# Levels 2 to 4 of a triangular inverse as one finite series, in a two-layer hybrid decoder on one Trainium2 core

## What is computed

```python
def step(state, inp):
    rt, wt, kt, vt, kkt, at = inp
    sa = jnp.einsum('bhvk,bhk->bhv', state, -kkt)
    state = state * wt[:, :, None, :] + sa[..., None] * (kkt * at)[:, :, None, :] + vt[..., None] * kt[:, :, None, :]
    return state, jnp.einsum('bhvk,bhk->bhv', state, rt)
```

```python
s = jnp.einsum('bhcqd,bhckd->bhcqk', q[:, :, :, q0:kend], k[:, :, :, :kend]).astype(jnp.float32) * scale
p = jax.nn.softmax(jnp.where(mask, s, -jnp.inf), axis=-1)
w = p[:, :, 0] - lam * p[:, :, 1]
```

## Time and profile before

| what | value |
|---|---|
| three runs | 2528.36, 2528.58, 2529.15 us |
| profiled execution | 2529.05 us, its span 2527.2 us |
| PE busy | 99% of the span |
| DVE, ACT, POOL busy | 75%, 48%, 19% |
| mean granted TensorE clock | 0.997 |
| chain that ended last | PE 94%, DVE 3%, issue 1%, ACT 1% |
| idle of PE before transposes (L1438) that wait for DVE L1149 | 2.3 us in 8 times |
| one even step (L1475 at 112.42 us to L1475 at 165.24 us) | 52.82 us |

### The profile page before, as it was taken

One profiled execution on the slowest core, in us unless ns is written; L12 is line 12 of the kernel. 1 busy time (PEld: TensorE's weight loads), 2 busy tenths in 40 slices (PEclk: granted clock), 3 DMA queues, 4 the chain that ended last, 5 costly groups with the idle time before them and its releaser, 6 DMA issues.

```text
span 2527.2 us, 49529 instructions
## 1 busy us (share of the span) xinstructions
PE 2495.7 (99%) x18082; PEld 2223.5 (88%) x18082; DVE 1883.5 (75%) x3163; ACT 1202.7 (48%) x1717; POOL 468.8 (19%) x360
## 2 busy tenths in 40 slices
PE   8999999999999999999999999999999999999998
PEld 8999998788888888888888888888888888888887
DVE  7888888776665666566889999997666566755776
ACT  6555455454333343343556565655434334333345
POOL 0011000132210221022221212223222012200223
PEclk9999999999999999999999999999999999999999
DMA  7333332355555555555554444445555555555543
GB/s 269 111 128 121 136 115 99 143 185 189 191 189 194 183 188 194 184 190 183 175 200 155 177 151 177 153 155 205 186 186 190 192 183 193 188 186 193 188 166 133
DMA packets 66006, 437.36 MB, mean 173 GB/s; under 512 B 9456, under 2 KB 10864, under 8 KB 17904
## 3 DMA queue, kind: packets, MB, share of 16 engines
q1 hardware_dynamic: 62064, 435.25, 48.8%
q10 hardware_dynamic: 3840, 0.70, 0.1%
HBM read 433.82 MB, written 2.10 MB: 172 GB/s over the span
## 4 chain that ended last, share of the span: by engine, by line
PE 94%; DVE 3%; issue 1%; ACT 1%; POOL 0%; DMA 0%; DVEq 0%; SPq 0%; POOLq 0%; ACTq 0%
PE acc L324 51%; PE acc L376 21%; PE acc L359 9%; PE acc L321 7%; DVE w_low L314 1%; PE mixer_banks L1438 1%; PE mixer_banks L1726 0%; PE mixer_banks L1548 0%; PE mixer_banks L1730 0%; PE acc L336 0%; PE mixer_banks L1525 0%; PE mixer_banks L1496 0%; PE mixer_banks L1489 0%; POOL arena L528 0%; DMA w_raw<-w_even 0%
## 5 line engine op out<-in xcount | busy, mean ns | idle before, releaser
L309 ACT ACTIVATE w_high<-w_raw 128x1024 fp32r<-128x1024 f32 x839 | 855.0, 1056 | 887.2 <-PE acc L376 746.2
L314 DVE TENSOR_TENSOR w_low<-w_raw,w_high 128x1024 fp32r<-128x1024 f32 x840 | 1058.9, 1291 | 19.4 <-ACT w_high L309 17.9
L324 PE MATMUL acc<-h_split,w_high 128*128 128x512 f32 x3840 | 944.7, 393 | 0.0
L324 PEld LDWEIGHTS acc<-h_split,w_high 128*128 128x128 f32 x3840 | 700.2, 189 | 131.2
L504 POOL TENSOR_TENSOR arena<-arena,norm_scale 128x256 f32<-128x256 f32 x152 | 232.3, 1528 | 1354.3 <-DVE arena L398 1335.6
L324 PE MATMUL acc<-mix_split,w_high 128*128 128x512 f32 x1904 | 463.0, 393 | 0.8 <-DVE x_residual L966 0.7
L324 PEld LDWEIGHTS acc<-mix_split,w_high 128*128 128x128 f32 x1904 | 348.0, 189 | 67.0 <-issue 1.7
L398 DVE TENSOR_REDUCE arena<-acc 128x256 f32<-128x512 f32 x240 | 165.5, 690 | 286.3 <-PE acc L376 270.0
L376 PEld LDWEIGHTS acc<-h_split,w_low 128*128 128x128 f32 x2752 | 352.8, 192 | 13.4
L376 PE MATMUL acc<-h_split,w_low 128*128 128x256 f32 x2752 | 357.1, 283 | 0.0
L359 PE MATMUL acc<-h_split,w_low 128*128 128x256 f32 x1824 | 276.4, 283 | 0.0
(11 more groups left out here) (289 smaller groups left out, 1600.6 us busy)
## 6 DMA issues: line engine op xcount, KB each, us to landing
w_raw<-w_gu SPq DMA_DIRECT2D x176, 1024.0 KB, 4.8
w_raw<-w_down SPq DMA_DIRECT2D x64, 1024.0 KB, 4.9
w_raw<-w_odd SPq DMA_DIRECT2D x64, 1024.0 KB, 4.8
w_raw<-w_even SPq DMA_DIRECT2D x49, 1024.0 KB, 4.8
w_raw<-w_down SPq DMA_DIRECT2D x32, 768.0 KB, 4.2
w_raw<-w_odd_out SPq DMA_DIRECT2D x12, 1024.0 KB, 4.8
w_raw<-w_even_out SPq DMA_DIRECT2D x10, 1024.0 KB, 4.7
w_raw<-w_even_out SPq DMA_DIRECT2D x6, 896.0 KB, 4.4
```

The source lines that it names most:

```text
L309: act.activation(wh[:, self.res, ks], raw[:, self.raw, ks], ACT.Copy).then_inc(high_done, 1)
L314: dve.tensor_tensor(wl[:, self.res, ks], raw[:, self.raw, ks], wh[:, self.res, ks].bitcast(F32), ALU.subtract).then_inc(low_done, 1)
L324: pe.matmul(acc[self.acc][:, 0:2 * T], wh[:, self.res, k], flat(both), start=k == 0, stop=stop)
```

## The change

In even steps levels 2 to 4 become one finite series. Let X be minus the inverse of the 4x4-block part times the rest of L within the 32x32 blocks. X is nilpotent, its eighth power is zero, and so the inverse is (I + X)(I + X²)(I + X⁴) times the start. `z(2)` makes X from one mask (`C_OVER`, the sum of the three masks of levels 2 to 4). `txt(2)` and `txt(3)` each hold two groups of 16 products: one squares the power (`pe.matmul(bank(1)...Xb...Zs)`), one multiplies T. `txt(4)` is one group. `z(3)` and `z(4)` are gone. DVE transposes each power before its square (`power_turned`), and T is only transposed back after level 4. POOL lays on two masks instead of four. The dense pieces are 5, 6, 6, 6, 6, 4, 3, 3, 3 tiles instead of 5, seven times 4, 3, 3, 3: 42 in both. `kbT` moves from ahead of a dense piece to between `z(6)` and R0, `at_oT` from behind `txt(5)` to behind `txt(6)`, and the banks of `kbn`, R0, U0 and `at_oT` change.

```diff
@@ POOL
                 pool.wait_ge(S["rw_L"], 4 * j + 4)
-                for l in range(1, LEVELS - 2):
...
-                    pool.tensor_tensor(Xb[:, l % 2], Ld, bc(half_mask(l), 4), ALU.mult).then_inc(S["rw_X"], 1)
+                pool.wait_ge(S["rw_TXT"], 5 * j)
+                pool.tensor_tensor(Xb[:, 1], Ld, bc(half_mask(1), 4), ALU.mult).then_inc(S["rw_X"], 1)
+                pool.tensor_tensor(Xb[:, 0], Ld, bc(cst[:, C_OVER:C_OVER + 32], 4), ALU.mult).then_inc(S["rw_X"], 1)
@@ ACT
                 def z_copy(l):
-                    act.wait_ge(S["rw_Z"], 5 * j + l - 1)
+                    if l in (3, 4):
+                        act.wait_ge(S["rw_TXT"], 5 * j + l - 2)
+                    else:
+                        act.wait_ge(S["rw_Z"], 3 * j + max(1, l - 3))
...
                 z_copy(2)
+                z_copy(3)
...
-                z_copy(3)
...
                 act.activation(flat(avn), bank(4)[:, 0:256], ACT.Copy).then_inc(S["at_vn"], 1)
+                z_copy(4)
                 high(8)
                 high(9)
-                z_copy(4)
+                z_copy(5)
...
-                z_copy(5)
                 high(11)

                 act.wait_ge(S["rw_kbT"], j + 1)
-                act.activation(flat(kbn), bank(5)[:, 0:256], ACT.Copy).then_inc(S["rw_kbn"], 1)
+                act.activation(flat(kbn), bank(4)[:, 0:256], ACT.Copy).then_inc(S["rw_kbn"], 1)
@@ DVE
+                def power_turned(p):
+
+                    dve.wait_ge(S["rw_Zs"], 5 * j + p)
+                    dve.transpose(Xb[:, 1], Zs).then_inc(S["rw_TT"], 1)
...
                     if l < LEVELS - 2:
-                        dve.tensor_tensor(TT[:, :, 0], TT[:, :, 0], bank(0)[:, 0:P].rearrange("p (n c) -> p n c", n=4), ALU.subtract).then_inc(S["rw_TT"], 1)
-                        dve.wait_ge(S["rw_TT"], 8 * j + l)
-                        dve.transpose(TT[:, :, 1], TT[:, :, 0]).then_inc(S["rw_TQ"], 1)
+                        at = P if l == 3 else 0
+                        dve.tensor_tensor(TT[:, :, 1], TT[:, :, 1], bank(0)[:, at:at + P].rearrange("p (n c) -> p n c", n=4),
+                                          ALU.subtract if l == 2 else ALU.add).then_inc(S["rw_TQ"], 1)
+                        if l == 4:
+                            dve.wait_ge(S["rw_TQ"], 4 * j + 4)
+                            dve.transpose(TT[:, :, 0], TT[:, :, 1]).then_inc(S["rw_TT"], 1)
                         return
...
                 level(2)
+                power_turned(2)
                 evacuate(1)
                 low(6)
+                level(3)
+                low(7)
...
-                level(3)
-                low(7)
+                level(4)
                 evacuate(2)
+                low(8)
@@ PE
+                    if l < 4:
+                        pe.wait_ge(S["rw_TT"], 8 * j + l)
+                        for n in range(4):
+                            for r in QUARTERS:
+                                at = P * (3 - l) + 32 * n
+                                pe.matmul(bank(1)[r, at:at + 32], Xb[r, 1, n], Zs[r, n], start=True, stop=True)
...
                 z(2)
-                dense(4)
+                dense(6)
                 txt(2)
...
-                dense(4)
-                z(3)
-                dense(4)
+                dense(6)
                 txt(3)
-                dense(4)
-                z(4)
+                dense(6)
+                txt(4)
+                dense(6)
+                z(5)
...
                 z(6)
+                transposed(bank(4)[:, 0:P], bk[:, 1, 0:P])
+                transposed(bank(4)[:, P:2 * P], bk[:, 0, 0:P]).then_inc(S["rw_kbT"], 1)
                 waits(pe, 2 * j + 2, "rw_KTR")
                 pe.wait_ge(S["rw_kbn"], j + 1)
...
                 dense(3)
                 txt(6)
+                pe.wait_ge(S["at_on"], j + 1)
+                for q in range(2):
+                    last = transposed(bank(5)[:, q * P:(q + 1) * P], on[:, q])
+                last.then_inc(S["at_oT"], 1)
                 dense(3)
```

More of the change, by code:

```diff
@@ L41 @@
 C_QUART = C_IDQ + 32
-C_END = C_QUART + P
+C_OVER = C_QUART + P
+C_END = C_OVER + 32
 P_MU, P_W0, P_A0, P_KK, P_KA, P_RK = 0, 3, 4, 5, 6, 7
@@ L72, in shape_constants @@
     c[:, C_HALF + 64:C_HALF + 96] = c[:, C_HALF:C_HALF + 32] + c[:, C_HALF + 32:C_HALF + 64] + c[:, C_IDQ:C_IDQ + 32]
+    c[:, C_OVER:C_OVER + 32] = c[:, C_HALF + 96:C_HALF + 192].reshape(P, 3, 32).sum(1)
     c[:, C_QUART:C_QUART + P] = s // 32 == t // 32
@@ L1075, in even_step @@
                 dve.stream_shuffle(lower, upper, THIRD).then_inc(S["rw_T0"], 1)
-                dve.wait_ge(S["rw_X"], 4 * j + 1)
+                dve.wait_ge(S["rw_X"], 2 * j + 1)
                 dve.wait_ge(S["rw_T0"], made + 4)
@@ L1114, in even_step @@
                     dve.tensor_tensor(prob[:, c], bank(4 + c)[:, 0:384], cst[:, C_CAUSAL:C_HALF], ALU.add).then_inc(S["at_sm"], 1)
+                power_turned(1)
                 dve.wait_ge(S["at_sm"], 2 * j + 2)
@@ L1143, in even_step @@
                     dve.tensor_tensor(KTR[:, 2 * n:2 * n + 2], bank(2 + n).rearrange("p (a b) -> p a b", a=2), tri, ALU.mult).then_inc(S["rw_KTR"], 1)
-                level(4)
-                low(8)
+                level(5)
                 low(9)
@@ L1152, in even_step @@
                 evacuate(3)
-                level(5)
+                level(6)
+                low(11)
                 dve.wait_ge(S["at_oT"], j + 1)
-                dve.tensor_scalar(atmp, bank(4)[:, 0:256], gn[:, G_SUB:G_SUB + 1], None, ALU.mult).then_inc(S["at_out"], 1)
+                dve.tensor_scalar(atmp, bank(5)[:, 0:256], gn[:, G_SUB:G_SUB + 1], None, ALU.mult).then_inc(S["at_out"], 1)
                 dve.wait_ge(S["at_out"], 2 * j + 1)
@@ L1159, in even_step @@
                 dve.tensor_tensor(ml[:, j], atmp, mh[:, j].bitcast(F32), ALU.subtract).then_inc(S["at_end"], 1)
-                low(11)
-                level(6)
                 low(12)
@@ L1521, in z @@
                         return
-                    pe.wait_ge(S["rw_X"], 4 * j + l)
+                    pe.wait_ge(S["rw_X"], 2 * j + 2)
                     for n in range(4):
                         for r in QUARTERS:
-                            last = pe.matmul(bank(1)[r, 32 * n:32 * n + 32], Xb[r, l % 2, n], TT[r, n, 0], start=True, stop=True)
+                            last = pe.matmul(bank(1)[r, 32 * n:32 * n + 32], Xb[r, 0, n], TT[r, n, 0], start=True, stop=True)
                     last.then_inc(S["rw_Z"], 1)
@@ L1545, in txt @@
                         return
+                    if l < 4:
[4 more added lines that the diff above has]
+                                pe.matmul(bank(1)[r, at:at + 32], Xb[r, 1, n], Zs[r, n], start=True, stop=True)
                     for n in range(4):
                         for r in QUARTERS:
-                            last = pe.matmul(bank(0)[r, 32 * n:32 * n + 32], TT[r, n, 1], Zs[r, n], start=True, stop=True)
+                            at = P * (l == 3) + 32 * n
+                            last = pe.matmul(bank(0)[r, at:at + 32], Zs[r, n], TT[r, n, 1], start=True, stop=True)
                     last.then_inc(S["rw_TXT"], 1)
@@ L1572, in even_step @@
                 dense(4)
-                txt(4)
+                txt(5)
                 waits(pe, j + 1, "at_wt", "at_vn")
@@ L1577, in even_step @@
                 pe.matmul(bank(5)[:, P:2 * P], wt[:, 2 * P:3 * P], avn[:, 1], start=False, stop=True).then_inc(S["at_o"], 1)
-                dense(4)
-                z(5)
-                dense(4)
-                txt(5)
-                pe.wait_ge(S["at_on"], j + 1)
-                for q in range(2):
-                    last = transposed(bank(4)[:, q * P:(q + 1) * P], on[:, q])
-                last.then_inc(S["at_oT"], 1)
-                transposed(bank(5)[:, 0:P], bk[:, 1, 0:P])
-                transposed(bank(5)[:, P:2 * P], bk[:, 0, 0:P]).then_inc(S["rw_kbT"], 1)
                 dense(3)
                 z(6)
+                transposed(bank(4)[:, 0:P], bk[:, 1, 0:P])
+                transposed(bank(4)[:, P:2 * P], bk[:, 0, 0:P]).then_inc(S["rw_kbT"], 1)
                 waits(pe, 2 * j + 2, "rw_KTR")
@@ L1593, in even_step @@
                 for h in range(2):
-                    last = pe.matmul(bank(5)[:, 256 + 64 * h:320 + 64 * h], KTR[:, 2 * h, 0:P], Vn[:, 0, 64 * h:64 * h + 64], start=True, stop=True)
+                    last = pe.matmul(bank(3)[:, 64 * h:64 * h + 64], KTR[:, 2 * h, 0:P], Vn[:, 0, 64 * h:64 * h + 64], start=True, stop=True)
                 last.then_inc(S["rw_R0"], 1)
@@ L1602, in even_step @@
                 for h in range(2):
-                    last = pe.matmul(bank(5)[:, 384 + 64 * h:448 + 64 * h], Tf[:, 2 * h], nR[:, 0, 64 * h:64 * h + 64], start=True, stop=True)
+                    last = pe.matmul(bank(3)[:, P + 64 * h:P + 64 * h + 64], Tf[:, 2 * h], nR[:, 0, 64 * h:64 * h + 64], start=True, stop=True)
                 last.then_inc(S["rw_U0"], 1)
```

11 lines of the change are left out of this document (4 added, 7 removed).

## The result

The changed kernel takes 2533.72 us, the median of 16 runs (2532.2 to 2535.94), the kernel before 2527.99 us in the same comparison: ratio 1.0024, 95% interval 1.0017 to 1.0032. The forecast was no change, 2528.7 us, with a range of 2524 to 2533 us. The measured time lies 0.7 us above that range, and a slowdown was measured that is small, 0.24%, but clear of the noise. The profiled execution took 2535.68 us, its span 2533.9 us.

What follows compares the result with a forecast made beforehand. PE, busy 99% of the span, was taken as the bound. Steps 0 to 6 at +0.7 us and step 7 at -0.6 us gave +0.1 us, so 2528.7 us, no change, with a range of 2524 to 2533 us.

Steps and rivals of the forecast that it cites:

- Two groups fewer, -0.58 us a step: PE, even steps: small-product groups interrupt dense work at four places instead of six; merging saves 0.29 us twice.
- The rival that groups in a row save nothing: PE, txt(2) and txt(3): the second group costs as much as one alone, 0.57 us; 2533.3 us, chance 5%.
- The two waits that go, -0.38 us: PE, even steps: the wait for `at_on` goes, -0.27 us, and z(6)'s wait for DVE's level 5, -0.11 us.
- low(6), +0.21 us: PE waits a step for low(6), which DVE does after level(2) and the second power_turned; from 0 to 0.5 us.
- R0, +0.82 us: PE's R0 must sit through ACT's copy of the keys (`kbn`) each step; from 0.69 to 1.1 us.
- The rival in which the keys' copy is covered: At R0: ACT's copy is done when PE gets there, so no 0.82 us wait; 2522.5 us, chance 10%.
- low(8) behind POOL, hidden: DVE after level(4): POOL's two operations take 1.55 us, then low(8) ends before PE needs it, hidden by 0.2 us.
- the rival built on it: POOL's two operations take 2.52 us by themselves, delaying low(8) by 0.73 us each step; 2534.9 us, chance 10%.
- The sign given for it, a step above 53.5 us: Even-step time in the profile after: above 53.5 us would show DVE's weight halves have become PE's bound.
- The sum for steps 0 to 6, +0.1 us each: Steps 0 to 6: -0.58 - 0.38 + 0.21 + 0.82 = +0.07 us; taken as 0.1 each, +0.7 us for seven.
- only its passes: PE: a second group directly behind another in the same shape taken as 0.28 us, bounds 0.26 and 0.38.
- Step 7, -0.6 us: Step 7: waits that go -2.1, groups -0.6, residual chain +1.0, low(6) +0.4, low(8) +0.5, R0 +0.2 us.

Runs made afterwards that it cites:

- the run that removes it: DVE's evacuate(1) and low(6) moved ahead of level(2), against the changed kernel padded at the start with R0 not awaiting the keys' copy: 2520.81 us, ratio 0.9972.
- 0.87 by the run: R0's wait for the keys' copy removed, against the changed kernel with 128 padding instructions at the start: 2522.97 us, ratio 0.9980 to the kernel before.

## Why the prediction was wrong

**Two groups fewer, -0.58 us a step: right but for the hole.** The second group in a row costs 0.29 us against 0.28 forecast, in txt(2) and, in the runs without holes, in txt(3). The rival that groups in a row save nothing gave 2533.3 us, near the measured time, but by a mechanism that the trace refutes; the agreement is chance.

**The two waits that go, -0.38 us: right.** No wait for `at_on` is left on PE, and z(6) starts 1.24 us behind the dense start at 149.54, against 1.37 before.

**low(6), +0.21 us: right in kind, 0.27 by the run that removes it. R0, +0.82 us: right.** 0.79 to 0.85 by the rows, 0.87 by the run. The rival in which the keys' copy is covered is out with it.

**low(8) behind POOL, hidden: right**, and the rival built on it is out: L526 took 1.68 us, not 2.52. The sign given for it, a step above 53.5 us, did come up in six steps, but from another cause.

**The sum for steps 0 to 6, +0.1 us each: right for the work that it counts.** The changed kernel without its holes, padded or with later or shorter loads, has steps of 52.92 to 52.94 us against 52.82.

**The step that failed is the one that took the second group's cost to be "only its passes", and put nothing down for the supply of instructions.** By its bounds the second group could cost 0.26 to 0.38 us. In txt(3) it cost its 0.29 us and 0.12 to 1.06 us of standing still. Packing 128 instructions of txt(2) and 128 of txt(3), with six tiles between, into 4.1 us brought two edges of the program's blocks to 3.83 us from each other, and the term "the loads are issued as DVE frees buffers; no weight half moves by over 2.2 us" looked at transfers only as carriers of weights. That they also delay PE's own program was in no term: 5.3 us of holes. The page before the change had the line for it, the queue "instruction" with its 71 transfers, and the time for a block, 6.1 us before, could have been counted. The Trainium skill (Runtime: NRT & Kernel Launch, Instruction fetch mechanics) gives the block as 16 KiB or 256 instructions; the transfers of 16 KB and the holes 1280 entries apart agree. It takes the fetch to be hidden, since instructions are issued more slowly than the memory is filled; here that held only where no weight transfer delayed the fetch or the block lasted long enough, 6.1 us before the change.

**Step 7, -0.6 us: wrong in size and sign.** It went from 54.54 to 54.69 us. U0 came 0.39 us earlier in the step (L1617 at 477.63, 40.91 us after its start, against 41.30), but then PE waited 0.4 us for S0 (PE's row first, then two of DVE's):

```profile
480.60 0.49 PE L1631 MATMUL mixer_banks<-arena 128*128 128x128 f32 x2 [0.37 <-DVE arena L1177]
476.41 0.42 DVE L1118 TENSOR_SCALAR arena<-mixer_banks 64x256 f32<-64x256 f32 x1 [1.20 <-PE mixer_banks L1546]
480.20 0.35 DVE L1177 SCALAR_TENSOR_TENSOR arena<-mixer_banks,small,constants_sb 128x128 f32<-128x128 f32 x1
```

DVE was idle until txt(6), and between level 6 (L1118) and S0 (L1177) it has two weight halves and the three operations on the attention's output, which `at_oT` now hands over only behind txt(6). Before, these three stood ahead of level 6, and DVE waited for PE at S0. The prediction had S0's slack worked out for step 1 only.

In sum: 5.3 us of holes, 0.8 us for the other 0.12 us in seven steps and 0.15 us in step 7 are 6.3 us of the 6.7 by which the spans differ; the rest lies ahead of step 0 and behind step 7 and varies from profile to profile (step 0 began between 59.45 and 61.2 us in kernels with the same work ahead of it or none added in its way).

## What to carry to other kernels

Instructions are a resource of PE as time is: count how many it works off between two block edges, above all where many small products stand together, and look at what the DMA queues carry when the next block must be fetched. A hole labelled "issue" inside a run of equal matmuls, behind the same pass in each repetition, is a sign of it. Here 128 instructions of padding or issuing the weights one wait later removed it (but for one hole in step 6 with the later loads), while 8, 32 and 240 instructions moved it and left most of it. The padding cost nothing where PE waited anyway: the kernel before took 2527.11 us with it and 2527.13 without. And when a product changes its bank, look whether the waits in front of it still protect anything: one of them was worth 6 us here.

## What the runs showed of the hardware

- PE's program arrives in transfers of 16 KB, one for 256 instructions, and a wait counts as an instruction.
- Such a transfer took 0.9 to 1.4 us in most cases (up to 1.9), and behind every hole its instructions ran 2.15 to 2.45 us after it began.
- A transfer of 1 MB of weights, some 3.5 us long, delayed it: in the changed kernel it began 1.8 to 2.6 us behind the edge and within 0.1 us of the transfer's end, and within 0.45 us of the edge where the transfer had been moved or cut. In the kernel before it could begin in mid-transfer, 1.9 us behind the edge.
- Small products from one group to the next in the same shape follow without a break, 32 passes in 0.27 us; that is 64 instructions, so by estimate a block of them alone would last 1.1 us.
- POOL and a DVE operation with two SBUF inputs took turns: the weight half took 2.61 us beside 1.68 us of POOL, which had started 0.16 us earlier, instead of 1.2 us.
